# Two decay buffers, a new order of convolutions, chunk outputs and routing, and gathers four experts ahead in one hybrid encoder layer

## What is computed

```python
h = rms_norm(x, norm_mix); z, xbc, dt_raw, q, k, v, u = split(h @ w_in)
y_ssd  = ssd_heads(...)        # conv of 4 taps + silu, two scans in chunks of 128, gate silu(z), norm
y_na   = neighbourhood_attention(q, k, v, ...)          # 4 heads, softmax over a window
y_pool = multiscale_pool(u, ...)                        # windows 2, 4, 8, 16
x = x + concat([y_ssd, y_na, y_pool]) @ w_out
x = x + memory_cross_attention(rms_norm(x, norm_xa), rms_norm(mem, norm_mem), ...)
x = x + hier_moe(rms_norm(x, norm_ffn), ...)            # group top 1, then top 2 of 8 experts, 32 in all
```

## Time and profile before

| | us |
|---|---|
| median of 3 runs | 1177.94 (1177.21 to 1178.67) |
| profiled execution | 1178.37 |
| its span, first to last instruction | 1176.3 |
| TensorE busy | 1016.5 (86%), mean granted clock 0.939 |
| VectorE busy | 787.0 (67%) |
| ScalarE busy | 470.6 (40%) |
| GpSimd busy | 300.4 (26%) |

### The profile page before, as it was taken

How to read it: one execution, slowest core, us unless ns; L and a number is a source line. 1 busy time by engine, 2 the same in 40 slices (tenths; PEclk the granted TensorE clock), 3 DMA queues, 4 the chain that set the end, 5 groups by cost and what they waited for, 6 DMA issues and landing times.

```text
span 1176.3 us, 13975 instructions
## 1 busy us (share of the span) xinstructions
PE 1016.5 (86%) x5029; PEld 812.8 (69%) x5029; DVE 787.0 (67%) x1251; ACT 470.6 (40%) x849; POOL 300.4 (26%) x346
## 2 busy tenths in 40 slices
PE   4898798998898999999979999666999888988883
PEld 3676586867677778788867888555777666766662
DVE  5437776776677677862355676457988777777771
ACT  5123353323234424421234333224666565555650
POOL 2223214321341222200111111004353333333312
PEclk9899999897898989899989999867999999999997
DMA  6132233121132523325210113735999999999952
GB/s 227 46 108 63 81 105 104 46 81 54 54 98 66 168 81 126 108 69 191 59 56 18 55 55 131 286 137 196 360 375 367 346 346 351 344 350 349 356 211 89
DMA packets 63396, 197.40 MB, mean 168 GB/s; under 512 B 16416, under 2 KB 22976, under 8 KB 50912
## 3 DMA queue, kind: packets, MB, share of 16 engines
q1 hardware_dynamic: 43344, 152.73, 36.1%
q0 software_dynamic: 18688, 39.52, 9.4%
q10 hardware_dynamic: 1296, 4.26, 0.9%
HBM read 190.16 MB, written 37.75 MB: 194 GB/s over the span
## 4 chain that ended last, share of the span: by engine, by line
PE 42%; DMA 13%; DVE 12%; issue 9%; ACT 4%; POOL 4%; ACTq 0%; POOLq 0%; DVEq 0%
DMA xg<-ffn_rows,idh 13%; PE bank L946 7%; PE bank L947 6%; PE bank L948 6%; PE gu_ps L946 3%; PE gu_ps L947 3%; PE gu_ps L948 3%; PE y_ps L1327 2%; PE bank L1131 2%; PE bank L1013 2%; PE xg_ps L1292 1%; ACT dec L1573 1%; ACT prob L1591 1%; PE bank L1263 1%; PE bank L1218 1%
## 5 line engine op out<-in xcount | busy, mean ns | idle before, releaser
L946 PE MATMUL bank<-Wh,hTh 128*128 128x512 f32 x384 | 160.0, 417 | 7.9 <-issue 6.7
L1728 DVE TENSOR_TENSOR egl<-egr,ghi 128x2048 fp32r<-128x2048 f32 x64 | 144.0, 2288 | 24.8 <-ACT ghi L1397 24.8
L947 PE MATMUL bank<-Wl,hTh 128*128 128x512 f32 x384 | 154.8, 403 | 0.0
L948 PE MATMUL bank<-Wh,hTl 128*128 128x512 f32 x384 | 154.0, 401 | 0.0
L1397 ACT ACTIVATE ghi<-egr 128x2048 fp32r<-128x2048 f32 x64 | 119.2, 1919 | 0.0
L946 PE MATMUL gu_ps<-ghi,xgH 128*128 128x512 f32 x256 | 104.4, 408 | 1.4 <-DVE xgL L2093 1.4
L948 PE MATMUL gu_ps<-ghi,xgL 128*128 128x512 f32 x256 | 101.3, 396 | 0.0
L947 PE MATMUL gu_ps<-egl,xgH 128*128 128x512 f32 x256 | 101.1, 395 | 0.0
L946 PEld LDWEIGHTS bank<-Wh,hTh 128*128 128x128 f32 x384 | 76.0, 198 | 24.8 <-issue 7.4
L948 PEld LDWEIGHTS bank<-Wh,hTl 128*128 128x128 f32 x384 | 75.2, 196 | 16.7
L947 PEld LDWEIGHTS bank<-Wl,hTh 128*128 128x128 f32 x384 | 75.4, 196 | 15.8 <-issue 0.8
(11 more groups left out here) (325 smaller groups left out, 2222.5 us busy)
## 6 DMA issues: line engine op xcount, KB each, us to landing
egr<-w_e_gate SPq DMA_DIRECT2D x32, 1024.0 KB, 16.6
egr<-w_e_up SPq DMA_DIRECT2D x32, 1024.0 KB
edr<-w_e_down SPq DMA_DIRECT2D x32, 1024.0 KB, 20.7
raw<-w_in SPq DMA_DIRECT2D x50, 256.0 KB, 3.0
xn<-w_in SPq DMA_DIRECT2D x22, 256.0 KB, 3.0
x_sb<-x_prompt SPq DMA_DIRECT2D x8, 512.0 KB, 6.0
partial_rows<-x_sb ACTq DMA_DIRECT2D x8, 512.0 KB, 2.6
ffn_rows<-xn_ffn POOLq DMA_DIRECT2D x8, 512.0 KB, 2.9
```

The costliest lines, as they stand in the source:

```text
L946: pe.matmul(dst, ah, bh, start=first, stop=False)
L947: pe.matmul(dst, ah, bl, start=False, stop=False)
L948: return pe.matmul(dst, al, bh, start=False, stop=last)
L1728: tt(egl[n % 4][:, a, :, :], egr[n % 4][:, a, :, :], ghi[n % 2][:, a, :, :].bitcast(F32), ALU.subtract)\
```

## The change

- **Start.** `hT(2)` and `hT(3)` of the first tiles move: the first projection comes after `hT(2)`, and `hT(3)` behind it. TensorE waits for the derived constants at `("dtp", 0)`, not at `("init",)`. The load of the first norm's gain is issued behind the first weights.
- **Convolutions.** The first tap runs on ScalarE, and the product after the tanh is a step of its own, `act`, which is placed later. `na1(0)`, the gates `z` and the convolutions get a new order; `dtv` is parted in `dtv` and `dtw`.
- **Scans.** There is a second buffer `dec1`, on the place of `prob`; `sdec(c)` waits for `sy(c-2)`. `ssd_groups` has ten groups for nine; `xdt` and `yn` are steps of their own; `yn(c)` and `sout(c)` come directly before `sdec(c+2)`. In `sy`, the output comes ahead of the state.
- **Routing.** The gain of the ffn norm is multiplied into the router's weights, `hT(ffn)` reads `x_sb`, and the row's scale is applied to the logits. The last two tiles have an order of their own, and VectorE copies half of the last `hT`.
- **Experts.** `gather_rows(n+4)` stands where `gather_rows(n+3)` stood; there are three `xg` buffers as before.

```diff
         z, norm, h_t = [("z", "z", i) for i in tiles], [("norm", st, i) for i in nxt], [("hT", st, i) for i in nxt]
-        mixed([[u[0]], [conv[4], na1[0]], [conv[5], conv_t[4]] + (ssd_groups(s - 1)[-1] if s else []),
-               [na2[0], u_t[0], u[1], nav[0]]], quarters(u0 + U_XS))
-        mixed([[na1[1], conv[0]], [conv[1], conv_t[0], na2[1]]], quarters(u0 + U_Z))
-        tl += [u_t[1], ("dtv", s), norm[0], conv[2], nav[1], conv_t[1], na1[2], norm[1], conv[3], conv_t[2]]
-        mixed([[z[0], h_t[0], na2[2]], [z[1], h_t[1], norm[2], nav[2], na1[3]],
-               [z[2], h_t[2], ("dt", s), conv_t[3], norm[3], na2[3]], [z[3], ("sback", s, 3), nav[3], h_t[3]]],
+        act = [("act", s, m) for m in range(6)]
+        mixed([[u[0], na1[0]], [conv[4]], [act[4], conv[5], conv_t[4]] + (ssd_groups(s - 1)[-1] if s else []),
+               [act[5], na2[0], u_t[0], u[1], nav[0]]], quarters(u0 + U_XS))
+        mixed([[conv[0]], [act[0], conv[1], conv_t[0]]], quarters(u0 + U_Z))
+        tl += [z[0], na1[1], act[1], conv_t[1], conv[2], u_t[1], na2[1], z[1], act[2], conv_t[2], norm[0], nav[1], ("dtv", s),
+               conv[3], na1[2], ("dtw", s), norm[1]]
+        mixed([[z[2], act[3], h_t[0], na2[2], ("dt", s)], [h_t[1], nav[2], norm[2], conv_t[3], na1[3]],
+               [z[3], h_t[2], norm[3], na2[3], ("sback", s, 3)], [("sback", s, 2), nav[3], h_t[3]]],
               quarters(u0 + 5 if s == 0 else U_MK))
...
-    back = [[("sback", s, 1), dec[0]]]
-    return back + [[y[0]], [dec[1], out[0]], [y[1]], [dec[2], out[1]], [y[2]], [dec[3], out[2]], [y[3]], [out[3]]]
+    groups = [[("sback", s, 1), dec[0], x[0]], [dec[1]]]
+    for c in range(TPS):
+        groups.append([y[c]] + x[c + 1:c + 2])
+        groups.append([yn[c], out[c]] + dec[c + 2:c + 3])
+    return groups
...
+    i = NT - 1
+    tl += [("xs2", i), ("hT", "ffn", i - 1), ("xav", i), ("topk", i - 2), ("norm", "ffn", i - 1), ("router", i - 1),
+           ("rank", i - 2), ("slots", i - 2), ("pre", 0), ("topk", i - 1), ("xo", i), ("rank", i - 1), ("hT", "ffn", i),
+           ("slots", i - 1), ("norm", "ffn", i), ("router", i), ("pre", 1), ("topk", i), ("rank", i), ("slots", i)]
...
-                if kind == "init":
+                if step == ("dtp", 0):
                     pe.wait_ge(const_ld, 16 * N_CONST)
...
+                    act.activation(cacc[:, k % 2, :], pb(step)[:, :], ACT.Identity, scale=cwh[:, m, 1:2],
+                                   bias=cbh[:, m:m + 1]).then_inc(conv_in, 1)
...
-                    if k:
-                        wait_full(dve, ("sy",) + chunks[k - 1], 0)
+                    if k > 1:
+                        wait_full(dve, ("sy",) + chunks[k - 2], 0)
...
-                if n + 3 < NE:
-                    gather_rows(n + 3)
+                if n + 4 < NE:
+                    gather_rows(n + 4)
```

More of the change, by code:

```diff
@@ L1463, in _ @@
                     i = step[2]
-                    for half in range(2):
+                    for half in range(1 if i == NT - 1 else 2):
                         wait_full(act, step, half)
@@ L1959, in _ @@
                     wait_transposed(dve, k)
+                    if s and m == 0:
+                        wait_full(dve, ("sy", s - 1, TPS - 1), 0)
                     for par in range(2):
```

145 lines of the change are left out of this document (87 added, 58 removed).

## The result

The changed kernel takes 1210.28 us (median of 4 runs, 1204.84 to 1213.18) against 1177.99; the ratio is 1.0267, with a 95% interval of 1.0248 to 1.0285. The forecast of 1161 and its range up to 1182 were wrong, on the side of the third rival. In the profiled execution the span is 1210.6 us after 1176.3: +34.3.

The account below looks back on a forecast made before the run. TensorE was taken to set the pace, VectorE close behind in strict order, with DMA limiting the experts. Terms -10 +2 +3 +4 +1 -3.9 -10 -3 = -16.9 took 1178.37 to 1161.5 us, 1161.0 as a median; 8-in-10 range 1132 to 1182.

Parts of the forecast that it names:

- third rival: Chunk scans: VectorE falls behind at `sout` in all eight chunks, not five; slower, 1186 us; chance 0.16.
- What bounds the kernel: Stages up to 522 us: TensorE, busy 85 to 95%, sets the pace; VectorE, 72 to 78%, follows in program order.
- Start: First tiles: the `init` wait is hidden behind matmuls already loaded; -10 us, bounds -7 and -10.5.
- Convolutions and gates: Two stages, 85 to 192 and 301 to 411 us: new waits replace old; +2 and +4, pair bounds -20 and +18.
- The chunk scans: 192 to 289 and 411 to 522 us: `dec` waits go, `sout` and bank waits come; +3 and +1.
- softmax stall: At `convT(1)`, behind `na1(1)`: TensorE has nothing for 7.4 us, then a slow clock of 1 to 2 us.
- Cross-attention and routing: Waits for the norm go in cross-attention, -3.9 us; `rank(7)` comes earlier, -10, bounds -4 and -13.
- Experts: Expert loop: DMA engines limit, so earlier gathers mostly lengthen the queue; -3 us, bounds 0 and -19.
- (1): Middle stages: the new waits are covered, -15 instead of +10, time 1136 us; chance 0.20.
- (2): Experts: DMA has room after all, share 0.98, -15 instead of -3, time 1149 us; chance 0.12.
- upper bound for the scans: Worst case for the scans of both sequences together: +21 us, against a lower bound of -18.
- range of 8 in 10: Whole kernel: 1132 to 1182 us, taking in the first, second and fourth rivals and the near half of the third.

Follow-up runs that it names:

- 1136.05 kernel: The changed kernel with the old order of convolutions and gates and the old order of the scan both put back: 1136.05 us, ratio 0.9635 to the kernel before.
- 1138.50: Second decay buffer alone, each decay one chunk earlier, all other orders as before, against the kernel with both orders put back (1136.05): 1138.50 us.
- stall experiments: Four TensorE stalls put into the output projection of the 1136.05 kernel: 1158.01 us; with 32 matmuls of 128x128 behind each stall: 1181.56 us.
- halved loads: The 1136.05 kernel with only the first half of each down-projection weight loaded from expert 4 on: 1110.07 us.

## Why the prediction was wrong, step by step

- **What bounds the kernel.** Right: TensorE sets the pace and VectorE, in strict order, is close behind. From this the third rival followed, and it was given too little.
- **Start.** Right: -10.2 for -10. The second projection ends at 32.0, and no wait stands near 27.
- **Convolutions and gates, +2 and +4; measured +7.2 and +17.4.** The new waits were found and sized: 7.37 for 7.4 at `convT(1)`, 2.01 for 2 at `convT(2)`, and in sequence 0 all idle time is 19.1 us after 16.0, for the 18 and 16 of the text. The failed terms are two. The slow clock was booked at some 2 us a stage; busy time rose by 4.1 and 6.4. And sequence 1 was costed with sequence 0's old waits: its idle time before was only 12.5, so there was less to take away, and 23.5 came.
- **The chunk scans, +3 and +1; measured +20.3 and +16.2.** This is the step that failed most, in two terms.
  First the waits. With 24.2 us of new ones and the 13.0 for `dec` gone, the text has TensorE idle for 11.2 us more in the two stages; measured are 24.4 (idle 10.9 to 23.1, and 5.3 to 17.5). Chunk 0 was right (7.33 for 8). Chunk 1, put at 0 twice, waited 3.9 and 5.0, in sequence 0 because of the weight quarter ahead of `yn`, which the text saw in sequence 1 only, and in sequence 1 because of the splits of the next input, as the trace reads, which it didn't see. Chunk 2 of sequence 0 waited 7.3 for 4, with `sy`'s own additions, a split and `yn` one after the other behind TensorE's last matmul. The bank behind two decays cost 8.0 for 4.5.
  Second, and larger, the clock. The text gave back 18 us of slow clock with the old waits, and what remains in its sum for the new ones, by subtraction, is 11: -7. Busy time in the two stages rose by 8.1 and 4.0: +12. No run shows that the waits for `dec` had cost 18. The order of before with them (the 1136.05 kernel) has TensorE busy 180.9 us in the two stages, and the order without them (1138.50) 178.5. That order has four other stalls in their place, so how the error parts between what was given back and what the new stalls cost stays open. The text priced a stall without asking what stands behind it; the real ones at `sout` have `sout`'s transposes and 32 decay matmuls, and cost 4.5 us (at 235.01) on top, where a softmax stall was priced at 1 to 2. In the stall experiments it was 1.8 to 2.2 ahead of a projection and 3.4 to 5.0 ahead of 32 short matmuls. These 19 us are over half of the 32.5 by which the two stages were off, the 13 of waits are the rest. The old order had fewer stalls: four at `dec`, against ten now.
- **Cross-attention and routing, -3.9 and -10; measured -18.6 from the first attention tile to the last `rank`.** Right, and the waits even in size: TensorE's idle time in this stretch fell by 14.7 us, for the 13.9 of the text. The rest, 4.0, is busy time, that is slow clock that went with the waits and wasn't in the sum. The last 55.08 us up to `rank`, first before, then after (0.73 in the earlier trace rows also takes in the wait behind it):

```profile
736.19:791.27 55.08, 35.11 (x183) 30.35 (x181) 27.82 (x95) 15.55 (x27) 4.06 (x9) 0.77 0.55 216
770.00:825.08 55.08, 45.97 (x262) 39.09 (x261) 37.81 (x126) 19.35 (x39) 6.59 (x14) 0.89 0.68 264
```

- **Experts, -3; measured +0.5 from the last `rank` on.** The reason was right, and shown by the halved loads: bytes bound them. The earlier gather gives 3.6 by itself. But what follows `rank` doesn't move forward by as much as a faster tail does: with the old gather and the new tail, `rank` to end takes 390.1 us, 5 more than before. A term for this was missing; that the first experts' loads are the reason isn't shown. The wait for rows turned into one for the down weights: ScalarE waits 94.5 us for them in the window from 940 to 1145, in which the gathers land after 23 us; in the same 205 us of the kernel before, 906 to 1111, it waited for no load.

```profile
ACT dhi L1404 <- DMA edr<-w_e_down: 94.5, 19, 5.5
...
edr<-w_e_down SPq DMA_DIRECT2D x19, 1024.0 KB, 26.0
xg<-ffn_rows,idh POOLq DMA_INDIRECT x18, 23.2
```

- **Rivals.** (3) is what happened, VectorE late at `sout` in all eight chunks, but its threshold was wrong: 5.3 us a chunk was to be needed, and 4.3 (34.6 in eight) were enough, since it had only "a little slow clock" in it. With all other terms as forecast, the +36.5 of the scans alone make +15.6; the rest of the +34.3 is the convolutions. Its 22.9 us also stand for six chunks, not five: 8, 4, 2.7, 2.5, 2.5, and 3.2 for the taps and `yn` behind the fifth convolution. (1) and (2) are out: none of the larger waits was covered, and the share in the experts is 0.93.
- **How the numbers follow.** The upper bound for the scans, +21, didn't hold the +36.5 that came, since it had no bound for the price of a stall in it, and the +18 for the convolutions didn't hold their +24.6. The parts that the range of 8 in 10 takes in add up to 0.92 of the chances, so it claimed more than its 0.8 and still missed. The bounds of the middle terms were set one by one, and the range took them as if they fell independently; but all of them hang on one thing, how late VectorE is, and on one price, that of a stall.

## What to carry to other kernels

A step that finishes a tile on a second engine (`yn`) and the step that consumes it on the first (`sout`) must not stand back to back in a shared order; put work of the first engine that needs nothing from the second between them, and the producer directly behind its own input. A second buffer for a producer gained nothing here, where the engine that fills it is busy 78% of the stage: the wait for the buffer only turned into one for what that engine does next. That its load is the reason isn't shown. Price a stall by what stands behind it: in these runs 1.8 to 2.2 us on top ahead of a projection, 3.4 to 5.0 ahead of short matmuls. A stall that goes away gives back a like price only if no other takes its place. Cheapest of all was to do first, within a step, what another engine waits for (the output ahead of the state, 9.7 us by the medians, 7.0 in the scan stages).

## What the runs showed of the hardware

- After stalls of 2.6, 4.6 and 7.2 us the time lost to the lower clock was about the same, 1.8, 2.2 and 2.2 us, with 128x512 matmuls behind them. With 32 matmuls of 128x128 first, those ran at 1.2 GHz from first to last behind the two longest stalls, 7.1 us for 3.8. Behind the two shortest, some 14 of them ran at 2.4 GHz before the clock fell, and the others at 1.2 to the last.
- The clock can fall after the wait is over. Behind the stall of 2.6 us alone, the first six matmuls of 128x512 came 0.23 to 0.26 us apart (the very first gap was 0.34), the next eight 0.38 to 0.43, and the others 0.23.
- A stall of 1.31 us left the clock at 1.00 when 128x512 matmuls followed, and was followed by 0.61 when 128x128 matmuls did.
- The core moved more than the 358 GB/s that the prediction cited from the Trainium skill (DMA: Bandwidth & Descriptors, Specifications) as its limit. In the 50 us from 900 to 950 of the changed kernel it was 372 at a share of 0.97:

```profile
900.00:950.00 50.00, 50.00 (x226) 38.30 (x224) 43.99 (x42) 31.71 (x40) 19.77 (x14) 1.00 0.97 372
```
